# Expert layer on one core: the u rows of the third tile's first two heads are gathered ahead of the ranks, later heads move up, and head 20's v rows are added on VectorE

## The reference

```python
def peer_ffn(h, w_q, sub_keys, u, v):     # h: (512, 1024); u, v: (16384, 1024)
    # per block of 128 tokens, 8 heads, k = 16
    q = (xt @ w_q).reshape(TOKEN_BLOCK, PEER_HEADS, 2, PEER_HALF_DIM)
    sc = jnp.einsum('thcd,chnd->thcn', q, sub_keys)
    top_s, top_i = lax.top_k(sc, k)
    ...
    idx = ...                              # 16 experts for each token and head
    g = jax.nn.softmax(best_s, axis=-1)
    pre = jnp.einsum('td,thkd->thk', xt, u[idx])
    coef = g * jax.nn.gelu(pre, approximate=False)
    return jnp.einsum('thk,thkd->td', coef, v[idx])
```

## Time and profile before

| what | value |
|---|---|
| median of three runs | 2225.74 us |
| the profiled execution | 2211.92 us |
| its span, first to last instruction | 2209.9 us |
| PE (TensorE matmul) busy | 1940.1 us, 88% of the span |
| DVE (VectorE) busy | 1383.5 us, 63% |
| POOL (GpSimd) busy | 934.9 us, 42% |
| ACT (ScalarE) busy | 547.1 us, 25% |
| bytes moved | 614.85 MB, mean 278 GB/s |

### The profile page before, as it was taken

How to read it: one execution, slowest core, us unless ns; L and a number is a source line. 1 busy time by engine, 2 the same in 40 slices (tenths; PEclk the granted TensorE clock), 3 DMA queues, 4 the chain that set the end, 5 groups by cost and what they waited for, 6 DMA issues and landing times.

```text
span 2209.9 us, 22139 instructions
## 1 busy us (share of the span) xinstructions
PE 1940.1 (88%) x7602; PEld 1231.5 (56%) x7602; DVE 1383.5 (63%) x3090; ACT 547.1 (25%) x1520; POOL 934.9 (42%) x814
## 2 busy tenths in 40 slices
PE   6999999887998998967778878899999999997776
PEld 5677666575865665544657666644457644442222
DVE  1111224455878874768986388899779966634554
ACT  2112024322111110212333237600138610011111
POOL 2000000010335562575761246533868864447775
PEclk9999998798998888986588889999999999999999
DMA  5322344155977797798875677899999999989998
GB/s 173 130 97 82 128 158 152 58 189 198 333 271 256 253 342 260 278 383 292 299 269 215 247 276 239 260 340 354 396 409 317 321 409 409 409 347 409 401 410 358
DMA packets 190623, 614.85 MB, mean 278 GB/s; under 512 B 18096, under 2 KB 18096, under 8 KB 190512
## 3 DMA queue, kind: packets, MB, share of 16 engines
q0 software_dynamic: 111168, 403.64, 49.6%
q1 hardware_dynamic: 76400, 202.92, 24.8%
q10 hardware_dynamic: 2944, 6.89, 0.9%
HBM read 610.22 MB, written 3.15 MB: 278 GB/s over the span
## 4 chain that ended last, share of the span: by engine, by line
PE 58%; DVE 12%; POOL 11%; issue 7%; DMA 7%; ACT 3%; ACTq 0%; POOLq 0%; SPq 0%; DVEq 0%
PE ps L1736 57%; POOL sb_arena L656 9%; DVE sb_arena L1206 4%; DMA sb_arena<-in_peer_u,sb_idx 3%; POOL sb_wring L656 2%; ACT sb_arena L1033 1%; DMA sb_wring<-in_w_out 1%; DMA sb_gains<-in_norm_g 1%; DVE sb_arena L1672 1%; PE ps L2054 1%; DMA sb_wring<-in_w_up_attn 1%; DMA sb_wring<-in_w_in 1%; DVE sb_arena L1346 0%; DMA sb_arena<-in_peer_v,sb_idx 0%; DVE sb_arena L1678 0%
## 5 line engine op out<-in xcount | busy, mean ns | idle before, releaser
L656 POOL DMA_INDIRECT sb_arena<-in_peer_u,sb_idx x470 | 602.8, 1283 | 1035.3 <-DVE sb_idx L1195 482.9
L1736 PE MATMUL ps<-sb_wring,sb_arena 128*128 128x512 f32 (+2 forms) x1632 | 699.5, 589 | 41.8 <-DVE sb_arena L1574 18.2
L1206 DVE CUSTOM_DVE_ANT_0 sb_arena<-sb_arena 128x1024 f32<-128x1024 f32 x470 | 562.4, 1222 | 102.0 <-DMA sb_arena<-in_peer_u,sb_idx 98.2
L1736 PEld LDWEIGHTS ps<-sb_wring,sb_arena 128*128 128x128 f32 x1632 | 312.6, 193 | 418.2 <-issue 365.5
L1736 PE MATMUL ps<-sb_arena,sb_wring 128*128 128x256 f32 (+2 forms) x2688 | 512.9, 353 | 14.6 <-ACT sb_arena L894 5.9
L1736 PEld LDWEIGHTS ps<-sb_arena,sb_wring 128*128 128x128 f32 x2688 | 447.8, 199 | 68.7 <-issue 6.5
L1736 PE MATMUL ps<-sb_arena 128*128 128x64 f32 (+9 forms) x1968 | 350.6, 330 | 57.9 <-DVE sb_arena L1678 16.8
L1736 PEld LDWEIGHTS ps<-sb_arena 128*128 128x128 f32 (+4 forms) x1968 | 279.6, 199 | 123.5 <-issue 73.8
L656 POOL DMA_INDIRECT sb_arena<-in_peer_v,sb_idx x192 | 202.8, 1056 | 121.3 <-PE ps L1736 50.3
L1736 PE MATMUL ps<-sb_arena,sb_poolw 128*128 128x512 f32 (+1 forms) x424 | 204.1, 608 | 56.6 <-DMA sb_arena<-in_peer_v,sb_idx 36.2
L1235 DVE SCALAR_TENSOR_TENSOR sb_arena<-sb_arena,sb_coef 128x1024 f32<-128x1024 f32 x90 | 115.5, 1284 | 118.3 <-DMA sb_arena<-in_peer_v,sb_idx 118.0
(11 more groups left out here) (240 smaller groups left out, 1341.3 us busy)
## 6 DMA issues: line engine op xcount, KB each, us to landing
sb_wring<-in_peer_v SPq DMA_DIRECT2D x128, 512.0 KB, 6.8
sb_wring<-in_w_in SPq DMA_DIRECT2D x52, 1024.0 KB, 7.5
sb_wring<-in_peer_w_q SPq DMA_DIRECT2D x32, 1024.0 KB, 7.4
sb_wring<-in_w_o SPq DMA_DIRECT2D x16, 1024.0 KB, 7.1
sb_wring<-in_w_out SPq DMA_DIRECT2D x8, 1024.0 KB, 9.3
sb_arena<-in_peer_u,sb_idx POOLq DMA_INDIRECT x470, 6.6
...
```

Source lines behind the costliest of these rows:

```text
L656: nc.gpsimd.indirect_dma_start(gathered[buf(n)], None, table, bass.IndirectOffsetOnAxis(ap=idx[:, t, at_:at_ + 1], axis=0))\
L1206: nc.vector.tensor_tensor_reduce(out=gathered[buf(n)], in0=gathered[buf(n)], in1=xn[:, t % TG, :], scale=1.0, scalar=0.0, op0=ALU.mult, op ...
L1736: return nc.tensor.matmul(o, l, r, start=start, stop=stop)
```

## The change

`EARLY_CHUNKS` goes from 16 to 18, and a new constant `DENSE_CHUNKS` = 16 stands wherever the old one meant the chunks whose v rows are computed with the whole table. So the u rows of chunks 16 and 17 are gathered into the six early buffers, and their dot products come before `split()`. All later u chunks move up by two: 18 is the chunk after the dense part (14 rows, `tops_of(20, 21)`, 2 rows), 19 and 20 stand beside the first builds, 21 to 26 beside the first dense tiles, 27 and 28 beside the second builds, 29 to 31 in `LATER`. `LATER` has v 19 and v 20 now, both wholly on VectorE (`ALL_VECTOR`), and `LAST` is 21 to 31. The v rows of chunks 16, 17 and 18 stay where they were. ScalarE's softmax and GELU steps and VectorE's `weigh` follow.

```diff
 EARLY_BUFS = 6
-EARLY_CHUNKS = 16
+DENSE_CHUNKS = TG * 8
+EARLY_CHUNKS = 18
...
-        V_FIRST, U_FIRST = 16, (17, 18)
+        V_FIRST, U_FIRST = DENSE_CHUNKS, (EARLY_CHUNKS + 1, EARLY_CHUNKS + 2)
         SHARED, V_SECOND = 18, 17
-        BY_VECTOR = head("u", 25) + head("v", SHARED, range(1, TOPK, 2)) + head("u", 26)
+        U_SECOND = EARLY_CHUNKS + 9, EARLY_CHUNKS + 10
+        BY_VECTOR = head("u", U_SECOND[0]) + head("v", SHARED, range(1, TOPK, 2)) + head("u", U_SECOND[1])
...
-        WITH_TILES = range(19, 25)
-        LATER = [("u", k) for k in range(27, CHUNKS)] + [("v", 19)]
-        LAST = range(20, CHUNKS)
+        WITH_TILES = range(EARLY_CHUNKS + 3, EARLY_CHUNKS + 9)
+        ALL_VECTOR = range(SHARED + 1, SHARED + 1 + 2)
+        LATER = [("u", k) for k in range(EARLY_CHUNKS + 11, CHUNKS)] + [("v", k) for k in ALL_VECTOR]
+        LAST = range(ALL_VECTOR[-1] + 1, CHUNKS)
...
         def on_vector(k, j):
-            return k == 19 or k not in (V_FIRST, V_SECOND) and j % 2 == 1
+            return k in ALL_VECTOR or k not in (V_FIRST, V_SECOND) and j % 2 == 1
...
                 for k in range(1 + H // 2, 2 * H):
                     yield from dots(k)
+                for k in range(DENSE_CHUNKS, EARLY_CHUNKS, 2):
+                    yield from tops_of(k, k + 1)
+                    yield from dots(k)
+                    yield from dots(k + 1)
                 split()
                 early_over[0] = True
-                yield from tops_of(2 * H, 2 * H + 1)
+                yield from tops_of(EARLY_CHUNKS, EARLY_CHUNKS + 1)
                 while not dense_over[0]:
                     yield
-                first_rows = dots(16)
+                first_rows = dots(EARLY_CHUNKS)
                 for _ in range(len(KEYS) + 4):
                     next(first_rows)
-                yield from tops_of(18, 19)
+                yield from tops_of(EARLY_CHUNKS + 2, EARLY_CHUNKS + 3)
...
-                pieces = tops_of(*range(20, 30))
+                pieces = tops_of(*range(EARLY_CHUNKS + 4, EARLY_CHUNKS + 12))
```

More of the change, by code:

```diff
@@ L1052, in _ @@
                 .then_inc(rank_copied, 1)
-            exp_soft(V_FIRST)
-            gelu(V_FIRST, V_FIRST + 1)
+            for k in range(V_FIRST, EARLY_CHUNKS):
+                exp_soft(k)
+            gelu(V_FIRST, EARLY_CHUNKS)
             act.wait_ge(rank_copied, 2)
@@ L1063, in _ @@
                 spread(b)
-            for k in range(17, 24):
+            for k in range(EARLY_CHUNKS, WITH_TILES[-1]):
                 exp_soft(k)
@@ L1074, in _ @@
                 spread(BUILDS + b)
-            for k in range(24, CHUNKS - 1):
+            for k in range(WITH_TILES[-1], CHUNKS - 1):
                 exp_soft(k)
@@ L1243, in finish @@
                 else:
-                    dve.wait_ge(v_used, sum(not on_vector(k, j) for k in range(EARLY_CHUNKS, H * t + H)
+                    dve.wait_ge(v_used, sum(not on_vector(k, j) for k in range(DENSE_CHUNKS, H * t + H)
                                             for j in range(TOPK)))
-                mine = sum(on_vector(k, j) for k in range(EARLY_CHUNKS, H * t + H) for j in range(TOPK))
+                mine = sum(on_vector(k, j) for k in range(DENSE_CHUNKS, H * t + H) for j in range(TOPK))
                 if t >= TG:
@@ L1304, in experts @@
                     pass
-                pieces = tops_of(*range(30, CHUNKS))
-                k_w = 23
+                pieces = tops_of(*range(EARLY_CHUNKS + 12, CHUNKS))
+                k_w = WITH_TILES[-1] - LAG
                 for kind, k in LATER:
```

13 lines of the change are left out of this document (7 added, 6 removed).

## The result

| | before | changed |
|---|---|---|
| median (range, runs), us | 2229.89 (2221.84 to 2240.43, 4) | 2269.15 (2264.2 to 2277.22, 4) |
| profiled execution, us (span) | 2211.92 (2209.9) | 2277.22 (2275.3) |

The ratio is 1.0177, with a 95% interval of 1.012 to 1.0234: +39 us, where the prediction had +16.9. The direction was right and the size was not: the time lies above the range (2224 to 2258). The four runs of before here have a median of 2229.89 us, 4.2 above the one that the forecast started from; so some 4 us of the distance to the forecast are before's. The two profiled executions differ by more than the medians (65.4 us in span), because the one of before was quick and the one of the changed kernel slow.

What follows compares the result with a forecast made beforehand. VectorE's first picks set the first build, TensorE then runs without slack, and row transfers bound the tail. Picks 37.6 us later less 20.7 of tail gave +16.9 us on 2225.74: 2242.6, range 2224 to 2258 (8 in 10).

Steps and rivals of the forecast that it cites:

- What bounds the kernel: TensorE follows the first build without slack up to 1964, VectorE sets that start; afterwards the tail lasts as its rows move.
- The tail, -20.7: Behind the dense tiles: 192 v rows become 176, 16 x 1.296 us each, 20.7 us off.
- Landing, 6.5 us: End of the attention: time from a gather's issue until VectorE can use its row, 6.5 us with DMA mostly idle.
- Rival B: Rows usable 3.2 us after issue; 17 dot products take 19.5, first picks about 27 us late, net +6.4: 2232; chance 0.14.
- Outputs +3.3 us: Attention's outputs on VectorE come 3.3 us later behind six dot products; everything up to the last norm follows.
- The six end at 1239.7: The six dot products ahead of the attention's outputs end at 1239.7; the outputs were at 1236.42 before.
- 17 dot products, 24 us: Behind the last norm: 17 dot products left, 19.5 us if bound by VectorE, 26.6 by six buffers; 24 taken.
- the room that looks free: From 1172 to 1237 VectorE is busy 32.84 of 65 us and the DMA share is 0.40.
- Chunk 18, 24.8 us: Rows issued only once their indices are written at 1300.8; the 14th row's dot product ends at 1325.6.
- The second selection, 15.6 + 2.3: Before the first picks: `tops_of(20, 21)` takes 15.6 us and two dot products 2.3, so `picks(0)` stands at 1343.5.
- Sum: First picks 37.6 us later less 20.7 from the tail: +16.9 us, 2242.6 on the median.
- rival C: Dot products inside the attention wait for rows, landing 10.3 us: `picks(0)` 51 us late, net +30, 2256; chance 0.18.

Runs made afterwards that it cites:

- after_again: The changed kernel, unedited, run again on another chip with a new profile: 2243.84 against 2206.78 us for the kernel before, ratio 1.0177.

## Why the prediction was right or wrong

- **What bounds the kernel: right.** The distance from the first build to the end of the dense tiles was 653.4 to 659.6 us in all the variants with early heads (655.6 before). What is late at the first build is late at the end.
- **The tail, -20.7: right in size** with the early heads in place (-16 to -22), but it took no account of what fits ahead of POOL's long wait: the gain is whole there, where 32 gathers had left the later stretch. Alone it is -5 to -10.
- **Landing, 6.5 us: too long.** The first dot product began 4.3 us after the issue (4.5 to 4.7 of waiting in seven profiles). The row with 6.5 us was the second of its burst, and the DMA engines' share was 0.99 while it landed (1965 to 1972); here it was 0.57 (1220 to 1224.2). The estimate of 3.2 us by the Trainium skill (DMA: Bandwidth & Descriptors, Anatomy of one DMA) was too short as well. Rival B fell for another reason too: the first dot product did end ahead of L1685's old time, as it said, but the 17 took 32 us, not its 19.5.
- **Outputs +3.3 us: too small.** "The six end at 1239.7" was 1242.5. The step reissued the buffers at once, while POOL took 1.7 to 2.0 us for an issue beside the dot products. The outputs were 5.5 to 5.8 us later than before, counted from the indices, and the last norm 6.8 to 7.7, not 3.3; the 1.0 to 2.2 us between the two are the projections at the lower clock, for which the sum had no term.
- **17 dot products, 24 us: the step that failed most.** 32 to 33, 8 us over the term. It named the weights that were still loading, but took VectorE and the six buffers for the two ends, where the DMA engines were full with rows and the weights of `peer_w_q` together. I had 26.6 from the earlier trace rows as the upper end and went below it. The stretch that the earlier trace rows is from shared the DMA engines too, but there 75.4% of their time went to the gathers (DMA page of before, 920 to 975 us, below); here it was 54 to 57%. The low DMA share of the earlier trace rows (0.40), which the prediction called the room that looks free, was that of 1172 to 1237, and the dot products stand behind 1264.

```profile
q0 software_dynamic: 4299, 15.66, 75.4%
q1 hardware_dynamic: 2083, 4.99, 24.3%
```

- **Chunk 18, 24.8 us: near.** 24.8 to 30.4. The first row came 5.1 to 7.8 us after its issue, and each dot product took 1.28 us instead of 1.146; where it was near 30 us, VectorE also waited 1.2 to 2.8 us for each of rows 2 to 5. (The prediction's own terms give 1324.2 for the landing, not 1324.4.)
- **The second selection, 15.6 + 2.3: right**, but for 3.1 us in the first profile, in which VectorE stood three times behind its own last instruction (0.70, 0.92 and 1.48 us). `after_again` has 15.2.
- **Sum.** `picks(0)` 50 to 58 us late instead of 37.6. For the second profile: first build 50.6 later, 1.8 more to the dense tiles' end, tail 18.8 shorter: 33.7 us, which is the difference of the spans (2243.6 - 2209.9); the medians differ by 37.1. That is near rival C's sum (51 late, net +30), but the agreement is luck: C reached it by a landing of 10.3 us inside the attention, which was 4.3. The range ended too soon because its upper end took the 17 dot products at 26.6 us at most.

Open stays what the 47.9 us on issue were, how much of chunk 18's scatter is DMA, and whether POOL or the DMA engines are what head 20's rows run short of when they move alone.
